# Seven products in place of eight for the right half of a branch projection, in a one-core hybrid block

## The chip, the cores and the metric

The kernel runs on one core of one Trainium2 chip. The metric is the device time of one execution, in microseconds. The engines named below are PE (TensorE, with PEld for its weight loads), DVE (VectorE), ACT (ScalarE), POOL (GpSimd) and SP (SyncE, which here only issues DMAs).

## What is computed

A block of a streaming encoder: 16 meta tokens and 256 frames of 2048 channels, float32, pass through an attention branch and a short-convolution branch; both are projected by a 2048x2048 matrix, gated, added and projected once more. The part that the change touches is `y_att`, the 256x2048 by 2048x2048 product.

```python
def hybrid_layer(x, norm_g, w_in, b_f, conv_w, w_att_o, w_conv_o, w_out):
    h = rmsnorm(x, norm_g)
    proj = jnp.einsum('bld,dn->bln', h, w_in)
    (q, k, v, f_logit, z_att, u, gate_b, gate_c, z_conv,
     m_att, m_conv) = jnp.split(proj, _split_points(), axis=-1)
    ...
    o_att = forgetting_attention(heads(q), heads(k), heads(v), log_f)
    y_att = jnp.einsum('blc,cd->bld', o_att * jax.nn.silu(z_att), w_att_o)
    o_conv = gate_b * short_conv(gate_c * u, conv_w)
    y_conv = jnp.einsum('blc,cd->bld', o_conv * jax.nn.silu(z_conv), w_conv_o)
    merged = jax.nn.sigmoid(m_att) * y_att + jax.nn.sigmoid(m_conv) * y_conv
    return x + jnp.einsum('bld,de->ble', merged, w_out)
```

## The kernel before

**Precision.** A float32 product is made of three matmuls: high part by high part, high by low, low by high. ACT rounds each weight to its high part (`round_unit`, the rows of L610), DVE subtracts to get the low part (`split_unit`, L934), PE does the three matmuls (`product`, L1478 to L1480; `wide_product` does the same work in two matmuls, L1492 to L1495).

**Units.** All weights come in units of 128x1024 floats (512 KB). A unit lands in one of 4 slots of `w_raw` by a DMA on SP's queue, is rounded into `w_hi` and split into `w_lo`, and is used by PE, which then counts up `w_used`. `w_hi` and `w_lo` each have room for 8 units (`RING`). During the convolution stage three of the eight hold other data (`quads`), so the ring has 5 slots (`CONV_RING`) up to unit `U_F`, and 8 from there on. A unit c may be rounded once the unit that held its slot before, c-8 (or c-5), is used: this is the wait on `w_used` in `round_unit`, with the value of `slot_reused(c)`. SP loads unit c once unit c-4 is split.

**Stages.** In the order of time: the convolution stage with six groups of gate columns done by Strassen's seven products (to 618 us), the forget gate and the convolution branch's projection (`U_WC`, to 706 us), the attention stage (`U_ATT`), the attention branch's projection (`U_WA`), the output projection (`U_OUT`), and the last norm.

**Attention stage.** Eight pairs of heads; each pair takes 12 units, 4 for K, 4 for Q and 4 for V. ACT and DVE go through the positions j = 1 to 12 of a pair: at each, first the rounding (ACT) or the split (DVE) of the unit that lies `LEAD` = 5 ahead, then whatever stands at that position. The work on the pair before (`finish_pair`) is hung into the next pair: PE transposes V after its first unit (j = 0), transposes the probabilities after its second, and after its fourth (j = 3) transposes z and multiplies V by the probabilities. ACT and DVE copy and split the transposed probabilities at position 3, and DVE then frees their banks (`free[C]`), for which PE's transposes of z wait. At position 5 DVE makes `gate`, `joined` and `prod2`, at position 6 the low part of `o`. At position 8 DVE adds up q (`join`) once PE has done 8 units, ACT rounds it, DVE makes `q_lo`, and PE waits for that (`q_split`) after its tenth unit, before the scores.

**Branch projection.** `natural` goes through four column blocks of 512 (`nb`), 8 units each; a unit is 2 tiles of k by 2 of tokens by 3 matmuls, 12 matmuls of 512 columns. The last pair of heads is finished inside the first block; its unit j waits for the low part of `o` of pair j (`o_split`). When a block is done DVE multiplies it by the gate and adds `partial` (`merged`), PE transposes the sum (`turn_m`, 8 transposes, after the second unit of the next block), and ACT and DVE round and split it for the output projection.

**Order.** The order on every engine is written out by hand; semaphores alone hold the engines together.

## Time and profile before

| what | value |
|---|---|
| median of 3 runs | 1209.2 us (1209.2 to 1209.27) |
| profiled execution, its own time | 1209.7 us |
| its span (first to last instruction) | 1207.9 us |
| PE busy | 1196.3 us, 99% |
| PE weight loads | 1070.2 us, 89% |
| DVE busy | 925.3 us, 77% |
| ACT busy | 651.9 us, 54% |
| DMA traffic | 280.40 MB, mean 232 GB/s |
| attention stage | 706 to 1018.8 us |
| branch projection of the attention | 1019 to 1112.4 us |

The profile is of one execution. A PE row's start is exact, its end is modelled, so the spacing of starts tells what a matmul costs. The waits that PE shows come to 4.5 us in all, none of them between 618 and 1112 us.

### The profile page before, as it was taken

What the parts mean: (1) busy time and instruction counts of PE and PEld (TensorE: products, weight loads), DVE (VectorE), ACT (ScalarE), POOL (GpSimd) and SP (SyncE); (2) the same over time, 40 slices, a digit from 0 to 9 for tenths busy, and PEclk for the clock granted to TensorE, in tenths of its full rate; (3) what the DMA queues carried; (4) which work ended last, traced back from release to release, by engine and by line L of the source; (5) the groups of instructions that cost most, each with busy time, mean ns of one, the idle gap of its engine ahead of it and who ended that gap; (6) DMA issues with size and microseconds to landing.
All of it is one profiled execution on the core that took longest, in us unless ns stands there. A gap on an engine that the chain in (4) does not pass through costs nothing.

```text
span 1207.9 us, 18425 instructions
## 1 busy us (share of the span) xinstructions
PE 1196.3 (99%) x7252; PEld 1070.2 (89%) x7252; DVE 925.3 (77%) x1095; ACT 651.9 (54%) x868; POOL 35.2 (3%) x50
## 2 busy tenths in 40 slices
PE   9999999999999999999999999999999999999997
PEld 8998898898888988889888899999999999888886
DVE  6989988988989989999966556767676667655544
ACT  7666555556656566656555445445544554543533
POOL 1000000000000000000000010111011101000000
PEclk9999999999999999999999999999999999999999
DMA  6788898898888898898678866556655655665663
GB/s 214 240 294 278 270 297 262 274 300 260 272 289 291 270 292 287 270 309 272 192 238 266 269 184 180 155 180 176 188 155 177 181 170 169 223 207 177 212 227 118
DMA packets 181249, 280.40 MB, mean 232 GB/s; under 512 B 9296, under 2 KB 128160, under 8 KB 180768
## 3 DMA queue, kind: packets, MB, share of 16 engines
q1 hardware_dynamic: 171760, 263.49, 68.3%
q10 hardware_dynamic: 9408, 15.78, 4.2%
q8 instruction: 57, 0.93, 0.3%
q14 instruction: 24, 0.20, 0.1%
HBM read 270.83 MB, written 8.41 MB: 231 GB/s over the span
## 4 chain that ended last, share of the span: by engine, by line
PE 87%; DVE 10%; issue 1%; ACT 1%; DMA 0%; ACTq 0%; POOLq 0%; POOL 0%; DVEq 0%
PE ps L1478 22%; PE ps L1480 22%; PE ps L1479 22%; PE ps L1494 7%; PE ps L1493 6%; PE ps L1495 3%; PE ps L1492 3%; DVE w_lo L1052 2%; DVE w_lo L1089 2%; DVE w_lo L1086 2%; DVE quads L1068 1%; DVE quads L1070 1%; DVE quads L1066 1%; DMA chan_rows<-in_norm_gain 0%; PE ps L1503 0%
## 5 line engine op out<-in xcount | busy, mean ns | idle before, releaser
L934 DVE TENSOR_TENSOR w_lo<-w_raw,w_hi 128x1024 fp32r<-128x1024 f32 x196 | 238.8, 1236 | 99.6 <-ACT w_hi L610 98.9
L1478 PE MATMUL ps<-h,w_hi 128*128 128x258 f32 (+1 forms) x1024 | 293.6, 287 | 1.4 <-DVE w_lo L1052 1.2
L1479 PE MATMUL ps<-h,w_hi 128*128 128x258 f32 (+1 forms) x1024 | 291.2, 284 | 0.0
L1480 PE MATMUL ps<-h,w_lo 128*128 128x258 f32 (+1 forms) x1024 | 290.9, 284 | 0.0
L610 ACT CAST w_hi<-w_raw 128x1024 fp32r<-128x1024 f32 x198 | 204.3, 1051 | 120.1 <-PE ps L1480 74.8
L1478 PEld LDWEIGHTS ps<-h,w_hi 128*128 128x128 f32 x1024 | 192.7, 188 | 5.4 <-issue 1.8
L1479 PEld LDWEIGHTS ps<-h,w_hi 128*128 128x128 f32 x1024 | 192.9, 188 | 2.1
L1480 PEld LDWEIGHTS ps<-h,w_lo 128*128 128x128 f32 x1024 | 192.8, 188 | 0.0
L1052 DVE TENSOR_TENSOR w_lo<-w_raw,w_hi 128x1024 fp32r<-128x1024 f32 x122 | 148.7, 1220 | 15.9 <-ACT w_hi L666 15.7
L1494 PE MATMUL ps<-h,w_hi 128*128 128x512 f32 x408 | 159.9, 397 | 1.0 <-DVE w_lo L1052 0.9
L666 ACT CAST w_hi<-w_raw 128x1024 fp32r<-128x1024 f32 x122 | 127.0, 1049 | 29.2 <-PE ps L1480 25.1
L1493 PE MATMUL ps<-h,w_hi 128*128 128x512 f32 x360 | 142.5, 396 | 0.0
L1495 PE MATMUL ps<-h,w_lo 128*128 128x256 f32 x408 | 113.4, 278 | 0.0
L682 ACT CAST w_hi<-quads 128x1024 fp32r<-128x1024 f32 x48 | 50.6, 1053 | 110.5 <-DVE quads L1068 105.0
L1492 PE MATMUL ps<-h,w_lo 128*128 128x256 f32 x360 | 100.3, 279 | 0.0
L1478 PE MATMUL ps<-w_hi,o 128*128 128x512 f32 x256 | 100.2, 391 | 0.0
L1480 PE MATMUL ps<-w_hi,o 128*128 128x512 f32 x256 | 99.7, 389 | 0.0
L1479 PE MATMUL ps<-w_lo,o 128*128 128x512 f32 x256 | 99.6, 389 | 0.0
L1495 PEld LDWEIGHTS ps<-h,w_lo 128*128 128x128 f32 x408 | 76.7, 188 | 14.7
L1494 PEld LDWEIGHTS ps<-h,w_hi 128*128 128x128 f32 x408 | 77.3, 190 | 6.1 <-DVE w_lo L1052 2.2
L1492 PEld LDWEIGHTS ps<-h,w_lo 128*128 128x128 f32 x360 | 67.6, 188 | 16.4
L1478 PE MATMUL ps<-w_hi,s_hi 128*128 128x512 f32 x192 | 75.1, 391 | 0.0
(211 smaller groups left out, 2055.2 us busy)
## 6 DMA issues: line engine op xcount, KB each, us to landing
w_raw<-in_w_in SPq DMA_DIRECT2D x226, 512.0 KB, 4.9
quads<-in_w_in SPq DMA_DIRECT2D x144, 512.0 KB, 4.5
w_raw<-in_w_conv_o SPq DMA_DIRECT2D x32, 512.0 KB, 5.7
w_raw<-in_w_att_o SPq DMA_DIRECT2D x32, 512.0 KB, 4.6
w_raw<-in_w_out SPq DMA_DIRECT2D x32, 512.0 KB, 4.5
quads<-in_w_in SPq DMA_DIRECT2D x48, 256.0 KB, 5.0
gates_dram<-stage ACTq DMA_DIRECT2D x24, 256.0 KB, 4.9
gate_nat<-gates_dram ACTq DMA_DIRECT2D x8, 512.0 KB, 4.1
```

The lines of the kernel that those rows point to most:

```text
L610: nc.scalar.copy(w_hi[:, hi_slot(c), :], w_raw[:, c % RAW, :]).then_inc(w_rounded, 1)
L666: nc.scalar.copy(w_hi[:, hi_slot(c), :], w_raw[:, n % RAW, :]).then_inc(w_rounded, 1)
L682: nc.scalar.copy(w_hi[:, hi_slot(c), :], quads[:, q, 0, :]).then_inc(w_rounded, 1)
L934: nc.vector.tensor_tensor(w_lo[:, lo_slot(c), :], w_raw[:, c % RAW, :], w_hi[:, hi_slot(c), :].bitcast(F32), ALU.subtract).then_inc(w_spli ...
L1052: nc.vector.tensor_tensor(w_lo[:, lo_slot(c), :], w_raw[:, n % RAW, :], w_hi[:, hi_slot(c), :].bitcast(F32), ALU.subtract).then_inc(w_spli ...
L1478: nc.tensor.matmul(dst, a_hi, b_hi, start=start, stop=False, skip_group_check=resumed)
L1479: nc.tensor.matmul(dst, a_hi, b_lo, start=False, stop=False, skip_group_check=resumed)
L1480: return nc.tensor.matmul(dst, a_lo, b_hi, start=False, stop=stop, skip_group_check=resumed)
L1492: nc.tensor.matmul(dst[:, HI, :], a_lo, b[:, HI, :], start=False, stop=False)
L1493: return nc.tensor.matmul(dst, a_hi, b, start=False, stop=stop)
L1494: nc.tensor.matmul(dst, a_hi, b, start=start, stop=False)
L1495: return nc.tensor.matmul(dst[:, HI, :], a_lo, b[:, HI, :], start=False, stop=stop)
```

## The change

The left half of the columns of `w_att_o` (two blocks of 512) is projected as before. For the right half, seven products take the place of eight: with two column blocks, two token tiles and pairs of k tiles as the 2x2 blocks, `WA_ORDER` has 16 units of the old kind (`n`, 12 matmuls each) and 28 new ones (`a`, `t1`, `b`, `t2`, `b22`, 6 matmuls each); the stage has 44 units where it had 32.

The sums that this needs are made in the attention stage. For each pair, SP loads 1 MB of `w_att_o` (`load_t`) behind the pair's first load, DVE makes four sums of 128x512 (`sum_t`: three at position 7, one at position 9), and SP stores the 1 MB to HBM (`store_t`). Of the activations DVE makes four sums of 128x128 at position 6 (`os_sum`), ACT rounds them at position 7, DVE makes their low part at position 8, and SP stores 512 KB for each pair (`store_os`); POOL's queue fetches seven of them (3.7 MB) when the attention stage ends. PE's first `t1` unit waits for that.

The sums lie where three slots of the `w_hi` ring were. So `hi_slot` and `slot_reused` now use 5 slots up to `U_WIDE`, half way through the output projection, in place of `U_F`; and in the attention stage and behind it the lead is 4 units (`LEAD_5`).

In the branch stage the gate of the first left block is still made at position 8 (`GATE_STEPS`), the first `merged` follows there, and PE transposes it after its unit 10 (`M_TURN`); the last two blocks are put together from the products (`combine`, `merge_products`) at the start of the output projection, whose order is now 8, 4 and 4 tiles of k for each half.

```diff
-OUT_STEP = 8
-OUT_K = OUT_STEP // 2
+
+U_WIDE = U_OUT + 16
...
 def hi_slot(c):
-    return (c - U_F) % CONV_RING if c < U_F else (c + 5) % RING
+    return (c - U_WIDE) % CONV_RING if c < U_WIDE else (c - U_WIDE + CONV_RING) % RING
...
 def slot_reused(c):
 
-    return RING + c - (CONV_RING if c < U_F else RING) + 1
+    return RING + c - (CONV_RING if c < U_WIDE else RING) + 1
...
+        M_TURN = (LEFT_END + 3, RIGHT_END + 4, N_WA + 2, N_WA + 4)
+        M_ROUND = (LEFT_END + 4, RIGHT_END + 5, N_WA + 3, N_WA + 5)
+        GATED = (LEFT_END + 1, RIGHT_END + 1, N_WA, N_WA + 3)
         CONV_STEPS = 4
         ATT_STEPS = 6
-        FIRST_GATE_LOAD, FIRST_GATE_STEP = 5, 8
+        LEAD_5 = LEAD - 1
...
+            def load_t(i):
+
+                if i > 1:
+                    sp.wait_ge(t_stored[i % 2], i // 2 * 16)
+                sp.dma_start(t_quads[:, i % 2, :, :, :], w_att_k[:, 2 * i:2 * i + 2, UNIT:D].rearrange(
+                    "p k (n c) -> p k n c", n=2)).then_inc(t_landed[i % 2], 16)
...
+            pool.wait_ge(w_used, RING + U_WA)
+            pool.wait_ge(os_stored, (PAIRS - 1) * 16)
+            nc.gpsimd.dma_start(os[:, 0:PAIRS - 1, :, :, :].rearrange("p i s n t -> p i (s n t)"),
+                                os_dram.rearrange("i p x -> p i x")).then_inc(os_landed, 16)
...
+                if j == 7:
+                    act.wait_ge(os_made, (i + 1) * 4)
...
+                    nc.scalar.copy(dst, os_sum[:]).then_inc(os_rounded, 1)
 
             for i in range(PAIRS):
                 for j in range(1, N_ATT + 1):
-                    round_unit(None, 0, U_ATT + i * N_ATT + j + LEAD)
+                    if i > 0 or j > 1:
+                        round_unit(None, 0, U_ATT + i * N_ATT + j + LEAD_5)
...
+                    nc.vector.tensor_tensor(os_sum[:, S1, :], a22, a21, ALU.subtract).then_inc(os_made, 1)
+                    nc.vector.tensor_tensor(os_sum[:, S3, :], a11, a21, ALU.subtract).then_inc(os_made, 1)
...
             for i in range(PAIRS):
                 steps = i * ATT_STEPS
                 for j in range(1, N_ATT + 1):
-                    split_unit(None, 0, U_ATT + i * N_ATT + j + LEAD)
+                    if i > 0 or j > 1:
+                        split_unit(None, 0, U_ATT + i * N_ATT + j + LEAD_5)
                     if i > 0:
                         finish_pair(i - 1, j)
+                    if j == 7:
+                        for part in range(3):
+                            sum_t(i, part)
+                    if j == 9:
+                        sum_t(i, 3)
...
+                elif kind == "a":
+                    product(p1, *o_piece(2 * first, 0), *w(left), **ends(first))
+                    last = product(p2, *o_piece(2 * first + 1, 0), *w(right), **ends(first))
+                elif kind == "t1":
+                    product(p5_, *os_piece(S1, 2 * first), *w(left), **ends(2 * first))
+                    last = product(p5_, *os_piece(S1, 2 * first + 1), *w(right), **ends(2 * first + 1))
+                elif kind == "b":
+                    product(p2, *o_piece(2 * first + 1, 1), *w(left), **ends(first))
+                    last = product(p7, *os_piece(S3, first), *w(right), **ends(first))
+                elif kind == "t2":
+                    product(p1, *os_piece(S2, 2 * first), *w(left), **more(2 * first))
+                    last = product(p1, *os_piece(S2, 2 * first + 1), *w(right), **more(2 * first + 1))
+                else:
+                    product(p5_, *os_piece(S4, 2 * first), *w(left), **more(2 * first))
+                    last = product(p5_, *os_piece(S4, 2 * first + 1), *w(right), **more(2 * first + 1))
```

How DVE's row of work changes in a pair of the attention stage, from the end of position 4 to `q_lo` (L939 and L1061 are `join` in the two files; `w_lo` rows are splits of units). Before:

```order
L1297 TENSOR_TENSOR k_lo<-ps,k_hi 128x544 [waits kq_rounded]
L934 TENSOR_TENSOR w_lo<-w_raw,w_hi 128x1024 [waits w_rounded]
L1273 SCALAR_TENSOR_TENSOR gate<-gate,ps 128x512 [waits z_tanh]
L939 TENSOR_REDUCE joined<-ps 128x512 [waits pv_done]
L1279 SCALAR_TENSOR_TENSOR prod_54<-joined,gate 128x512 [waits free_c,free_e]
L934 TENSOR_TENSOR w_lo<-w_raw,w_hi 128x1024 [waits w_rounded]
L1283 TENSOR_TENSOR o<-prod_54,o 128x512 [waits o_rounded]
L934 TENSOR_TENSOR w_lo<-w_raw,w_hi 128x1024 [waits w_rounded] x2
L939 TENSOR_REDUCE joined<-ps 128x512 [waits w_used]
L1305 TENSOR_TENSOR q_lo<-joined,q_hi 128x512 [waits kq_rounded,free_a]
```

Between the low part of `o` and `q_lo` on DVE there stood two splits and the `join`. Now, in DVE's row from the low part of `o` on:

```order
L1402 TENSOR_TENSOR o<-prod_54,o 128x512 [waits o_rounded]
L1407 TENSOR_TENSOR os_sum<-prod_54 128x128
L1408 TENSOR_TENSOR os_sum<-prod_54 128x128
L1410 SCALAR_TENSOR_TENSOR os_sum<-os_sum,prod_54 128x128 [waits os_made]
L1413 SCALAR_TENSOR_TENSOR os_sum<-prod_54,os_sum 128x128 [waits os_made]
L1056 TENSOR_TENSOR w_lo<-w_raw,w_hi 128x1024 [waits w_rounded]
L1427 TENSOR_TENSOR t_quads<-t_quads 128x512 [waits t_landed1]
L1429 TENSOR_TENSOR t_quads<-t_quads 128x512
L1432 TENSOR_TENSOR t_quads<-t_quads 128x512 [waits t_summed]
L1056 TENSOR_TENSOR w_lo<-w_raw,w_hi 128x1024 [waits w_rounded]
L1418 TENSOR_TENSOR os_pair<-os_sum,os_pair 128x512 [waits os_rounded]
L1061 TENSOR_REDUCE joined<-ps 128x512 [waits w_used]
```

Four sums of 128x128, three of 128x512 and one low part of 128x512 have come in ahead of the `join`; `q_lo` follows it as before.

On PE, the first transposes of `merged` in the branch stage stood between two units of the second block, after its second unit, behind 24 matmuls since the first block's end. Before:

```order
L1480 MATMUL ps<-w_hi,o 128x512
L1478 MATMUL ps<-w_hi,o 128x512
L1479 MATMUL ps<-w_lo,o 128x512
L1480 MATMUL ps<-w_hi,o 128x512
L1472 MATMUL ps<-ident,merged 128x128 [waits merged_made]
L1472 MATMUL ps<-ident,merged 128x128 x7
L1478 MATMUL ps<-w_hi,o 128x512 [waits w_split]
```

Now on PE they stand behind the first `t1` unit:

```order
L1672 MATMUL ps<-w_hi,os 128x512 [waits w_split,os_landed]
L1673 MATMUL ps<-w_lo,os 128x512
L1674 MATMUL ps<-w_hi,os 128x512
L1672 MATMUL ps<-w_hi,os 128x512
L1673 MATMUL ps<-w_lo,os 128x512
L1674 MATMUL ps<-w_hi,os 128x512
L1666 MATMUL ps<-ident,merged 128x128 [waits merged_made]
L1666 MATMUL ps<-ident,merged 128x128 x7
L1672 MATMUL ps<-w_hi,o 128x512 [waits w_split,free_b]
```

Between the first block's end and these transposes there are now three units of 6 matmuls: 18.

## Rows read from the trace of the kernel before

**Rows 1.** The page, part 1: busy us, share of the span, instructions.

```profile
PE 1196.3 (99%) x7252; PEld 1070.2 (89%) x7252; DVE 925.3 (77%) x1095; ACT 651.9 (54%) x868; POOL 35.2 (3%) x50
```

**Rows 2.** The waits of PE: total us, times, longest; first and last of four.

```profile
PE ps L1503 <- POOL ident L565: 1.9, 1, 1.9
...
PE ps L1589 <- DMA chan_rows<-in_norm_gain: 0.5, 1, 0.5
```

**Rows 3.** Windows: length, busy us of each engine, clock, DMA share, GB/s.

```profile
9.00:12.00 3.00, 3.00 (x16) 2.63 (x15) 1.68 (x6) 2.70 (x6) 0.56 (x2) 1.00 1.08 382
...
330.00:360.00 30.00, 30.00 (x178) 26.60 (x178) 25.20 (x31) 18.23 (x25) 0.00 (x0) 1.00 0.90 289
...
862.00:901.00 39.00, 39.00 (x293) 37.44 (x293) 26.49 (x34) 18.77 (x35) 3.86 (x4) 1.00 0.58 175
```

**Rows 4.** Timeline of PE in a branch unit: start us, us, engine, line.

```profile
1107.62 0.39 PE L1478 MATMUL ps<-w_hi,o 128*128 128x512 f32 x1
...
1111.70 0.39 PE L1478 MATMUL ps<-w_hi,o 128*128 128x512 f32 x1
```

**Rows 5.** Timeline of PE in one pair: third unit's start, z's transposes, scores.

```profile
867.84 0.37 PE L1478 MATMUL ps<-h,w_hi 128*128 128x272 f32 x1
...
873.86 0.60 PE L1678 MATMUL ps<-ident,z_nat 128*128 128x128 f32 x4
...
892.77 0.23 PE L1478 MATMUL ps<-k_hi,q_hi 128*128 128x144 f32 x1
```

**Rows 6.** Timeline of ACT in the same pair.

```profile
868.12 0.80 ACT L828 CAST probs_t<-ps 128x768 fp32r<-128x768 f32 x1 [1.08 <-PE ps L1670]
...
874.06 0.61 ACT L854 CAST k_hi<-ps 128x544 fp32r<-128x544 f32 x1 [3.26 <-PE ps L1480]
874.57 1.05 ACT L610 CAST w_hi<-w_raw 128x1024 fp32r<-128x1024 f32 x1
875.51 0.60 ACT L836 ACTIVATE gate<-ps 128x512 f32<-128x512 f32 x1
...
881.53 1.05 ACT L610 CAST w_hi<-w_raw 128x1024 fp32r<-128x1024 f32 x1 [0.58 <-PE ps L1493]
```

**Rows 7.** Timeline of DVE in the same pair.

```profile
870.72 0.40 DVE L1266 SCALAR_TENSOR_TENSOR p_tail<-ps,tail_row,p_tail 32x32 fp32r<-32x32 f32 x2
...
875.65 1.23 DVE L934 TENSOR_TENSOR w_lo<-w_raw,w_hi 128x1024 fp32r<-128x1024 f32 x1 [0.22 <-ACT w_hi L610]
...
878.64 0.69 DVE L1279 SCALAR_TENSOR_TENSOR prod<-joined,gate 128x512 f32<-128x512 f32 x1
879.25 1.53 DVE L934 TENSOR_TENSOR w_lo<-w_raw,w_hi 128x1024 fp32r<-128x1024 f32 x1
...
881.88 2.35 DVE L934 TENSOR_TENSOR w_lo<-w_raw,w_hi 128x1024 fp32r<-128x1024 f32 x2
887.05 1.22 DVE L939 TENSOR_REDUCE joined<-ps 128x512 f32<-128x1024 f32 x1 [2.81 <-PE ps L1493]
889.03 0.69 DVE L1305 TENSOR_TENSOR q_lo<-joined,q_hi 128x512 fp32r<-128x512 f32 x1 [0.76 <-ACT q_hi L857]
```

**Rows 8.** Groups by line: count, busy us, mean ns; small operations of DVE.

```profile
L1258 DVE TENSOR_TENSOR v_tail<-ps,v_tail 32x256 fp32r<-32x256 f32 x8 | 3.3, 416 | 0.1
...
L1319 DVE TENSOR_SCALAR nmax<-smax 128x4 f32<-128x4 f32 x8 | 1.4, 170 | 0.3
```

**Rows 9.** Timeline of DVE in the branch stage.

```profile
1036.57 0.69 DVE L1283 TENSOR_TENSOR o<-prod,o 128x512 fp32r<-128x512 f32 x1
...
1044.57 1.22 DVE L1243 TENSOR_TENSOR merged<-ps,gate_nat 128x1024 f32<-128x1024 f32 x1 [3.08 <-PE ps L1480]
1045.83 1.23 DVE L1356 TENSOR_TENSOR merged<-merged,partial 128x1024 f32<-128x1024 f32 x1
```

**Rows 10.** Timeline of ACT in the branch stage: position 8.

```profile
1039.18 1.05 ACT L610 CAST w_hi<-w_raw 128x1024 fp32r<-128x1024 f32 x1 [1.67 <-PE ps L1480]
...
1041.55 1.06 ACT L801 ACTIVATE gate_nat<-gate_nat 128x1024 f32<-128x1024 f32 x1
```

More of the change, by code:

```diff
@@ L102 @@
 HI, LO = 0, 1
-OUT_BANK = (4, 0)
+OUT_BANK = (0, 4)
 A, B, C, E = 0, 2, 4, 6
@@ L1358, in _ @@
-            split_m(NB - 1)
-            rest = UNITS - (U_OUT + 1 + LEAD)
-            with dve.Fori(0, rest // RING) as i:
-                for j in range(RING):
-                    split_unit(i, RING, U_OUT + 1 + LEAD + j)
-            for n in range(UNITS - rest % RING, UNITS):
-                split_unit(None, 0, n)
+                nc.vector.tensor_tensor(merged[:], ps[:, bank:bank + 2, :], gate_wa[:, nb, :, :], ALU.mult
+                                        ).then_inc(free[bank], 1)
```

373 lines of the change are left out of this document (285 added, 88 removed).

## The prediction, made before the changed kernel had run

> **What bounds the kernel now.** I read the page's shares first: PE is busy 99% of the span [rows 1]. Matmul busy time alone does not show that PE is at its limit, so the waits come next: PE waits 1.9 us for its first operand and 0.5 us for another at the start, 4.5 us in all, and in the attention and branch stages not once [rows 2]. A window of one pair in the attention stage shows PE busy all 39.00 us, DVE 26.49, ACT 18.77, DMA at 175 GB/s [rows 3]. So every matmul taken away shortens the kernel by its spacing, and every wait put on PE lengthens it by its length. DVE has a third of its time free, but that is an average: what counts is how early the results for which PE waits are made. The timelines of one pair [rows 5 to 7] tell that, so the prediction is made from them.
>
> **What is removed.** 18 matmuls of a branch unit start within 1107.62 to 1111.70 us, 0.2267 us each [rows 4]. Before, the right half took 16 units of 12, 192 matmuls; now 28 units of 6, 168. That is 24 x 0.2267 = **5.4 us less** on PE. No transposes come or go.
>
> **What the shorter ring does in the attention stage.** Before, at position j ACT rounded unit j+5 into a slot last held by the unit eight earlier. Now it rounds unit j+4 into a slot last held by unit j-1, five earlier (units counted from 0), and so cannot start position j before PE has ended unit j-1. Before, it could start when unit j-3 had ended. That this wait is real can be seen before the change: at 881.53 ACT starts a rounding released by PE, which is position 8 waiting for unit 5 [rows 6]. Everything that stands at a position now comes up to two units (5.5 us) later against PE. Two of PE's own waits depend on it.
>
> **First wait: the transposes of z (after PE's fourth unit).** They start at 873.86; two units before them started at 867.84, so a unit is 3.01 us and unit 2 ends at 870.85 [rows 5]. They need `free[C]`, freed by DVE at position 3, at 870.72 + 0.40 = 871.12, so 2.7 us of slack [rows 7]. After the change position 3 starts when unit 2 has ended. ACT follows PE by 0.20 (874.06 after 873.86 [rows 5, 6]); the rounding keeps it 0.94 (874.57 to 875.51); from its copy of the probabilities (868.12) to DVE's end at 871.12 are 3.00 [rows 6, 7]. The way back to PE I take as 0.08, an estimate between the 0.03 that DVE follows ACT by (874.57 + 1.05, then 875.65) and the 0.20 of PE to ACT. Sum 0.20 + 0.94 + 3.00 + 0.08 = 4.22, against one unit of 3.01: PE waits **1.21 us**, in 7 pairs, 8.5 us. The eighth time is in the branch stage, where a unit is 12 x 0.2267 = 2.72: 1.50 us.
>
> **Second wait: q for the scores (after the tenth unit).** ACT sees unit 5 end at 881.53 and DVE sees unit 7 end at 887.05, so a Q unit is 2.76 and unit 4's end was seen at 878.77; the scores start at 892.77, 14.00 after that [rows 5 to 7]. DVE's `q_lo` is ready at 889.03 + 0.69 = 889.72, slack 3.05. Now position 5 starts at unit 4's end, and DVE has work in one row from there: rounding and start of the split 1.08 (874.57 to 875.65); that split, gate, `joined`, `prod2`, the next split and the low part of `o` 6.23 (875.65 to 881.88); the four sums of 128x128; a split 1.22, of which 0.08 overlaps the next (as 0.69 takes 0.61 from 878.64 to 879.25), so 1.14; three sums of 128x512 at 0.61, 0.72 (the next one waits for its end) and 0.61, 1.94; a split 1.14; the low part of the sums 0.61; from the `join` to the end of `q_lo` 2.67 (887.05 to 889.72); 0.08 [rows 6, 7]. No row shows a 128x128 sum. It lies between a 128x4 operation, 170 ns, and a 32x256 one, 416 ns [rows 8]; by size nearer the middle, and I take 0.26 each with the waits between them, 1.05 (bounds 0.68 and 1.66). Sum 15.94, less 14.00: PE waits **1.94 us**, in the 7 pairs that have a pair before them, 13.6 us; by the bounds 11.0 to 17.9. The first pair has no pair to finish: from unit 6's end 1.08 + 1.14 + 1.94 + 1.14 + 2.67 + 0.08 = 8.05 against 14.00 - 2 x 2.76 = 8.48, no wait. Could these two waits hide each other? No: each is counted from a unit's end that is later than the wait before it.
>
> **Branch stage, two more.** The eighth unit waits for the low part of the last pair's `o`. From unit 4's end: 0.20 + 1.08 + 3.60 (875.65 to 879.25) + 1.14 + 0.69 [rows 9] + 0.08 = 6.79, against two units, 5.44: **1.35 us**. Then the first transposes of `merged`: position 8 starts at the first block's end; ACT's rounding, table load and gate take from 1039.18 to 1041.55 + 1.06 = 1042.61, 3.43 [rows 10]; DVE's two steps from 1044.57 to 1047.06, 2.49 [rows 9]; with 0.20, 0.03 and 0.08 the sum is 6.23. PE has only 18 matmuls to do, 4.08 us, where it had 24: it waits **2.15 us**. Together with the 1.50 above the branch stage gets 5.0 us of waits.
>
> **Edits at nothing.** Behind the last product DVE has its split, four combining steps and two of `merged`, ended 7.6 us after PE's last branch matmul (0.20 + 0.94 + a copy of 0.6, then 2.65 to 3.3 for the four sums at 0.69, then 2.5); PE transposes after three output units, 8.16, so 0.5 is spare. If that cover is gone the cost is what exceeds it. DMA in the attention stage: 2.5 MB more per pair is 64 GB/s on 175; the stage before ran at 289 with PE busy 30.00 of 30.00 [rows 3]. SP's stores stand behind loads that are issued four units after the sums are made, so they hold up no load; `load_t` is issued after position 4's split and has some 12 us to land (8 in the first pair). ACT's new copy, 0.6 us at position 7, ends before DVE's three sums do.
>
> **Sum.** -5.4 + 8.5 + 13.6 + 5.0 = **+21.7 us**. On the profiled execution: span 1207.9 to 1229.6, its time 1209.7 to 1231.4. The median of the runs is 0.5 lower, so 1209.2 + 21.7 = **1230.9 us**.
>
> **Rivals.**
> Only the first wait (1217.3 us). If DVE's row of work in positions 5 to 8 is 2 us shorter than summed, the second wait goes and its 13.6 with it. For it: 1.94 in 15.94 is a small difference of a long sum, and the split at 879.25 lasted 1.53 where others last 1.22 to 1.23 [rows 7], so some of the 6.23 is contention that may fall elsewhere. Against: four 128x128 sums at the least possible price still leave 1.6.
> All hidden (1203.8 us, faster than before). The mechanism is DVE's and ACT's spare third: the results for the z transposes and the scores are made within the slack they have now, 2.7 and 3.05 us, and the branch stage likewise. It decides at 3.01 us for the first chain, which I sum to 4.22, and at 14.00 for the second. For it: PE waits nowhere here before, and the 5.4 us are certain. Against: the ring's wait on `w_used` can be seen in [rows 6].
> Weights late as well (1234.6 us). A 6-matmul unit takes 1.36 us and 0.524 MB, 385 GB/s. At the 289 GB/s of the convolution stage [rows 3] a unit takes 1.81. The last 19 units (16 short, 3 long) and 8 transposes take PE 30.8 us; the loads 34.4, 3.6 more, less what the ring has ahead. POOL's 3.7 MB come in the first ten units. Against: three microseconds at 382 GB/s [rows 3], and eight units are ahead when the short ones begin. The Trainium skill, DMA: Bandwidth & Descriptors, Specifications, gives about 358 GB/s as the HBM limit of one core. By it 0.524 MB takes an estimated 1.46 us, 0.10 more than PE needs, and 28 units give at most 2.8 us; the row at 382 shows that this case has gone above that for 3 us.
>
> **Chances.** The forecast 0.57; only the first wait 0.18; weights late as well 0.14; all hidden 0.09; 0.02 for a result that happens to fall on no change. Range: with the bounds of the small sums the forecast is 1228.3 to 1235.2, with late weights up to 1239; the lower end takes in the 1217.3. I give 1215 to 1240, which leaves out the 1203.8 and 0.05 of mishaps. A difference under 0.2% is about what a measurement cannot tell from none: faster 0.09, within 0.02, slower 0.89.
>
> **What would show it.** PE's waits in the changed profile: the transposes of z waiting for DVE's `p_tail` 8 times at 1.2 to 1.5 us, the scores waiting for `q_lo` 7 times near 1.9, a branch matmul waiting once for `o`, the transposes of `merged` once near 2.1. A pair should take 3.15 us longer than before. ACT should wait for PE ahead of nearly every rounding. If a pair is only 1.2 longer, the second chain is mis-sized; if PE waits for `w_lo` in the short units, weights are late. The granted clock stays 1.00 in the windows if waits of this length leave it alone; a lower one would make the forecast too low.

## The result, and the profile after

The changed kernel takes 1252.6 us (median of four runs, 1250.4 to 1255.3) against 1209.2 before: ratio 1.036, 95% interval 1.034 to 1.038. The forecast was 1230.9 us with a range of 1215 to 1240. The direction was right. The size was wrong by 21.7 us, as much again as was forecast, and the time lies outside the range.

The profiled execution has a span of 1251.1 us, 43.2 more than before. Its page begins with the busy time of the engines, which answers to [rows 1]:

```profile
span 1251.1 us, 18110 instructions
## 1 busy us (share of the span) xinstructions
PE 1206.2 (96%) x7228; PEld 1074.8 (86%) x7228; DVE 973.7 (78%) x1184; ACT 672.1 (54%) x891; POOL 36.0 (3%) x51
```

PE issues 24 matmuls fewer and is nevertheless busy for 10 us longer. Waiting alone can't do that: waits show up in the idle time, not in the busy time. So two things happened, waits and slower matmuls. First the waits of PE (waiting line, what released it, us in total, times, longest), which answer to [rows 2]:

```profile
PE ps L1672 <- DVE q_lo L1461: 11.2, 7, 1.6
PE ps L1872 <- DVE p_tail L1385: 8.6, 7, 1.2
PE ps L1666 <- DVE merged L1501: 6.6, 3, 4.1
PE ps L1872 <- DMA z_nat<-gates_dram: 3.3, 1, 3.3
PE ps L1672 <- DVE left_c L1555: 1.5, 1, 1.5
PE ps L1672 <- DVE o L1402: 1.2, 1, 1.2
PE ps L1672 <- DVE w_lo L1056: 0.9, 1, 0.9
```

The first two rows and the sixth are waits of the forecast. The fourth, the fifth, the last and most of the third are not: a late transfer, a late product, a late weight, and a wait of 4.1 us where 0.5 us was said to be spare.

Then the windows (PE, PEld, DVE, ACT and POOL busy with counts, granted clock, DMA share, GB/s). The first is the pair of [rows 3], the other two follow one of the waits for `q_lo`:

```profile
862.00:901.00 39.00, 36.17 (x267) 34.20 (x266) 27.19 (x42) 19.20 (x34) 3.88 (x4) 1.00 0.70 227
952.00:954.00 2.00, 2.00 (x14) 2.00 (x13) 2.00 (x4) 0.00 (x0) 0.00 (x0) 0.66 0.38 57
954.00:956.00 2.00, 2.00 (x10) 2.00 (x10) 1.96 (x3) 0.00 (x0) 0.00 (x0) 0.50 0.97 312
```

In the first window, 39 of a pair's 43 us, PE is idle for 2.8 us, at full clock. Around 954 it is never idle, but the granted clock is 0.50, that is 1.2 GHz instead of 2.4, and 10 matmuls start in 2 us. The timeline of PE shows the change of pace (start, duration, line, operation, shapes; in brackets the idle time ahead and its releaser):

```profile
948.97 0.28 PE L1674 MATMUL ps<-h,w_lo 128*128 128x272 f32 x1
950.85 0.33 PE L1672 MATMUL ps<-k_hi,q_hi 128*128 128x144 f32 x1 [1.60 <-DVE q_lo L1461]
...
952.37 0.28 PE L1672 MATMUL ps<-h,w_hi 128*128 128x272 f32 x1
952.49 0.31 PE L1673 MATMUL ps<-h,w_hi 128*128 128x272 f32 x1
...
953.05 0.43 PE L1673 MATMUL ps<-h,w_hi 128*128 128x272 f32 x1
953.28 0.43 PE L1674 MATMUL ps<-h,w_lo 128*128 128x272 f32 x1
```

PE stood still from 949.25 to 950.85 and went on at full pace (0.12 us from one matmul to the next). From about 952.6 it needed 0.23 us for each. This happened six times while PE had work, each time for some 3.4 us, and each time at a wait: behind four of the seven waits for `q_lo` (at 778, 952, 997 and 1041), behind the wait for `z_nat` (1065), and from 1160.8 on, in the last half microsecond of the last wait for `merged`. Working through 3.4 us at half pace costs 1.7 us, so six cost some 10 us. In the profile before, the clock falls only after PE's last matmul.

The span divides like this; pairs are counted from one transpose of `v_t` to the next. The last pair's `v_t` is transposed from 1022.3 before and from 1052.0 now, the first pair's from 744.4 and 745.0:

| stretch | more than before | made of |
|---|---|---|
| up to the first pair's `v_t` | 0.6 | start-up and unchanged code; the profiles of all the kernels here differ by up to 2.6 |
| seven pairs | 29.1 | 7 x 3.2 of waits, 4 x 1.7 of half clock |
| last pair, branch, output | 13.5 | -5.4 of matmuls, 13.5 of waits, 2 x 1.7 of half clock, 2.0 more (seven waits, after which PE takes 0.2 to 0.3 to get going) |

The forecast had 22.1 for the second row and -0.4 for the third.

### The profile page after: what moved, and what is told of

It is laid out like the page before. It is cut to its first block, busy times and chain, and to the rows that moved or that the text cites. A ratio compares the mean times of both kernels' runs of the same rounds, so it can differ in the third digit from the quotient of the medians.

```text
span 1251.1 us, 18110 instructions
## 1 busy us (share of the span) xinstructions
PE 1206.2 (96%) x7228; PEld 1074.8 (86%) x7228; DVE 973.7 (78%) x1184; ACT 672.1 (54%) x891; POOL 36.0 (3%) x51
## 4 chain that ended last, share of the span: by engine, by line
PE 68%; DVE 20%; DMA 5%; ACT 4%; issue 2%; ACTq 0%; POOLq 0%; POOL 0%; DVEq 0%; SPq 0%
PE ps L1672 18%; PE ps L1674 17%; PE ps L1673 17%; PE ps L1688 5%; DVE w_lo L1056 4%; PE ps L1687 4%; PE ps L1689 3%; DMA w_raw<-in_w_att_o 2%; DVE w_lo L1174 2%; ACT w_hi L722 2%; PE ps L1686 2%; DVE w_lo L1211 2%; DVE w_lo L1208 2%; DVE joined L1061 1%; DVE quads L1190 1%
## 5 line engine op out<-in xcount | busy, mean ns | idle before, releaser
L1056 DVE TENSOR_TENSOR w_lo<-w_raw,w_hi 128x1024 fp32r<-128x1024 f32 x208 | 255.9, 1236 | 190.5 <-ACT w_hi L722 189.3
L722 ACT CAST w_hi<-w_raw 128x1024 fp32r<-128x1024 f32 x210 | 218.5, 1049 | 250.9 <-PE ps L1674 161.6
L1674 PE MATMUL ps<-h,w_lo 128*128 128x258 f32 (+1 forms) x1024 | 293.5, 287 | 0.0
L1672 PEld LDWEIGHTS ps<-h,w_hi 128*128 128x128 f32 x1024 | 195.5, 191 | 5.4 <-issue 1.8
L1673 PEld LDWEIGHTS ps<-h,w_hi 128*128 128x128 f32 x1024 | 195.6, 191 | 2.1
L1174 DVE TENSOR_TENSOR w_lo<-w_raw,w_hi 128x1024 fp32r<-128x1024 f32 x122 | 148.8, 1220 | 15.9 <-ACT w_hi L778 15.7
L778 ACT CAST w_hi<-w_raw 128x1024 fp32r<-128x1024 f32 x122 | 126.9, 1049 | 28.2 <-PE ps L1674 25.1
L1672 PE MATMUL ps<-w_hi,o 128*128 128x512 f32 x216 | 85.0, 393 | 2.7 <-DVE left_c L1555 1.5
L1673 PE MATMUL ps<-w_lo,o 128*128 128x512 f32 x216 | 84.3, 390 | 0.0
L1674 PE MATMUL ps<-w_hi,o 128*128 128x512 f32 x216 | 84.2, 390 | 0.0
L1688 PEld LDWEIGHTS ps<-h,w_hi 128*128 128x128 f32 x408 | 77.3, 190 | 6.1 <-DVE w_lo L1174 2.2
```

What stands on the lines that cost most here:

```text
L722: nc.scalar.copy(w_hi[:, hi_slot(c), :], w_raw[:, c % RAW, :]).then_inc(w_rounded, 1)
L778: nc.scalar.copy(w_hi[:, hi_slot(c), :], w_raw[:, n % RAW, :]).then_inc(w_rounded, 1)
L1056: nc.vector.tensor_tensor(w_lo[:, lo_slot(c), :], w_raw[:, c % RAW, :], w_hi[:, hi_slot(c), :].bitcast(F32), ALU.subtract).then_inc(w_spli ...
L1174: nc.vector.tensor_tensor(w_lo[:, lo_slot(c), :], w_raw[:, n % RAW, :], w_hi[:, hi_slot(c), :].bitcast(F32), ALU.subtract).then_inc(w_spli ...
L1672: nc.tensor.matmul(dst, a_hi, b_hi, start=start, stop=False, skip_group_check=resumed)
L1673: nc.tensor.matmul(dst, a_hi, b_lo, start=False, stop=False, skip_group_check=resumed)
```

## The experiments

### The ring alone

The kernel before, with the changed slot count and the lead of four, and nothing of the new products:

```diff
+U_WIDE = U_OUT + 16
-    return (c - U_F) % CONV_RING if c < U_F else (c + 5) % RING
+    return (c - U_WIDE) % CONV_RING if c < U_WIDE else (c - U_WIDE + CONV_RING) % RING
...
-                    round_unit(None, 0, U_ATT + i * N_ATT + j + LEAD)
+                    if i > 0 or j > 1:
+                        round_unit(None, 0, U_ATT + i * N_ATT + j + LEAD - 1)
```

> The kernel before with the shorter ring alone: five slots up to the sixteenth output unit, rounding one unit less ahead; no weight sums, no stores, the right half of the branch projection as before. Theory of the ring (waits come from positions that start up to two units later): the transposes of z wait 1.2 us in seven pairs and 1.5 us in the branch stage, the fifth wait in the branch stage 1.35 us, the first transposes of merged 0.8 us; the scores do not wait, since without the sums DVE's row from the end of the fifth unit is 12.3 us against 14.0. Sum 12.2 us, 1221.4 us. Theory of the clock: it fell only behind waits in the changed kernel; if a wait of 1.2 us is enough, some of these eight show half clock and up to 1.7 us more each comes on top; if only those of 1.6 us and more do it, the clock stays whole and the time is 1221. Rival (the waits come from DVE's sums, not from the ring): no waits and 1209 us.

Measured: 1222.9 us against 1208.8 in the same session, ratio 1.011 (1.010 to 1.013). PE's waits, and the window of a pair:

```profile
PE ps L1671 <- DVE p_tail L1262: 10.0, 8, 1.5
PE ps L1471 <- DVE o L1279: 1.2, 1, 1.2
PE ps L1465 <- DVE merged L1353: 0.7, 1, 0.7
```

```profile
862.00:901.00 39.00, 37.77 (x281) 36.03 (x280) 25.80 (x34) 18.94 (x34) 3.86 (x4) 1.00 0.52 162
```

All three waits of the ring stand there with the forecast sizes (10.0 for 8.5 + 1.5, 1.2 for 1.35, 0.7 for 0.8), and the scores don't wait. The granted clock stays whole throughout the attention and branch stages: none of the nine waits of 1.2 to 1.5 us was followed by half clock in this execution.

### A wait alone, in the kernel before

Is the half clock caused by PE standing still, or by something else in the changed kernel? Here only DVE gets more to do, so that PE waits 2 us in seven pairs:

```diff
+                        if i > 0:
+                            for n in range(7):
+                                nc.vector.tensor_tensor(q_lo[:], k_hi[:, :, 0:SEQ].bitcast(F32),
+                                                        k_hi[:, :, 0:SEQ].bitcast(F32), ALU.subtract
+                                                        ).then_inc(extra, 1)
+                                dve.wait_ge(extra, 7 * (i - 1) + n + 1)
                         join(bank, joined)
```

> The kernel before with one thing added: in seven pairs DVE does seven more operations of 128x512, each waiting for the one before (0.72 us apiece, 5.0 in all), between the end of q's projection and the join of q. q_lo has 3.05 us of slack, so PE waits 2.0 us seven times, 14 us in all, with the ring, the units and the transfers as before. Theory of the clock (half clock follows PE's standing still for about this long, sometimes): some of these seven waits are followed by half clock for some 3.4 us, at 1.7 us each: 1223 us and 0 to 12 us more, 1226 to 1233, with a spread from run to run. Rival (the dips of the changed kernel come from something else in it, its transfers or DVE's load): the clock stays whole and the time is 1223 in every run.

Measured: 1230.2 us (1229.3 to 1230.9) against 1210.1, ratio 1.017 (1.015 to 1.018). The wait, and windows behind two of the seven:

```profile
PE ps L1485 <- DVE q_lo L1312: 13.8, 7, 2.3
```

```profile
778.00:780.00 2.00, 2.00 (x13) 2.00 (x12) 1.97 (x3) 0.24 (x1) 0.00 (x0) 0.59 0.51 106
...
904.00:906.00 2.00, 2.00 (x14) 2.00 (x13) 2.00 (x2) 1.69 (x2) 0.00 (x0) 0.66 0.00 0
906.00:908.00 2.00, 2.00 (x11) 2.00 (x11) 1.97 (x4) 0.00 (x0) 0.00 (x0) 0.50 0.80 224
```

Three of the seven waits were followed by half clock, in a kernel that has neither the ring nor the new products nor their transfers. The window from 904 moved no bytes at all. The excess of 20.1 us is 7 x 2.15 of waiting and 3 x 1.7 of half clock.

### The same waits, filled

Sixteen transposes of the identity ahead of each of these waits; they touch nothing but the bank that the scores overwrite:

```diff
-                        pe.wait_ge(q_split, i + 1)
                         pe.wait_ge(free[C], FREE_C["att"] + 3 * i)
+                        if i > 0:
+                            for _ in range(16):
+                                nc.tensor.transpose(ps[:, C, 0:P], ident[:], ident[:])
+                        pe.wait_ge(q_split, i + 1)
```

> The kernel with the wait alone (d1_wait_alone), in which PE stood still seven times for 2 us and the clock halved three times, with sixteen transposes of the identity on PE ahead of each of these waits; at 0.11 us each they fill 1.8 of the 2.0 us, and the scores start at the same time as without them. Theory (half clock follows PE's standing still): no dip in the attention stage in the profiled run, and the time falls from 1230.2 by the three dips at 1.7 us, to 1225 us. Rival (the clock fell for DVE's added work or by chance): dips as before and 1230 us.

Measured: 1224.5 us (1224.4 to 1225.2) against 1208.9, as expected to half a microsecond.

```profile
PE ps L1485 <- DVE q_lo L1312: 1.6, 7, 0.5
```

The idle time at the scores went from 13.8 to 1.6 us, and the attention stage has no window under 1.00. The delay for the scores is still there, because DVE's added work is; only the half clock has gone. The seven pairs take 293.5 us against 298.1, 4.6 less, where three stretches were worth 5.1. The medians differ by 5.7, of which 1.2 is between the two sessions: the kernel before took 1210.1 in one and 1208.9 in the other. The four runs lie 0.7 us apart instead of 1.5.

### Fillers in the changed kernel

The same edit in the changed kernel, with twelve transposes.

> The changed kernel with twelve transposes of the identity on PE ahead of its wait for q_lo in seven pairs, written into the scores' bank before the scores. They fill some 1.4 to 1.8 us in which PE would stand still and nothing else is moved. Theory of the clock (half clock for 3.4 us follows PE's standing still): the dips at the scores, four of six in the profiled run, go, and the time falls by 4 x 1.7 = 6.8 us at most, less up to 0.2 us for each pair in which the fillers outlast the wait: 1246 to 1249 us, and closer together from run to run. Rival (the clock falls for a reason other than the wait): dips as often as before, 1252 or more.

Measured: 1247.7 us (1246.7 to 1250.5), 4.9 less than the changed kernel.

```profile
PE ps L1672 <- DVE q_lo L1461: 1.9, 7, 0.3
```

In the profiled execution no half clock is left at the scores; three stretches remain later, at the waits for `z_nat` (3.8 us here), for `left_c` (2.2) and for `merged` (3.8), and one stands at the start. The first of them is twice as long (6.8 us, 3.4 lost). So the seven pairs are 6.3 us shorter (300.7 for 307.0) and the rest is 2.2 longer (201.3 for 199.1), which is why the median gives only 4.9. The clock theory holds in both kernels.

### The weight sums behind q

```diff
-                    if j == 7:
+                    if j == 9:
                         for part in range(3):
                             sum_t(i, part)
-                    if j == 9:
+                    if j == 11:
                         sum_t(i, 3)
...
-                if j == 6 and 0 <= i - 1 < PAIRS:
+                if j == 8 and 0 <= i - 1 < PAIRS:
                     store_t(i - 1)
```

> The changed kernel with the four weight sums later in a pair: three at position 9 and one at 11, behind q_lo, and their store two loads later. Theory (the score wait is DVE's row of work between the end of the fifth unit and q_lo, of which the three sums are 1.94 us): the wait for q_lo falls from 1.6 us of idle time (1.9 by spacing) to at most 0.2, 13 us in seven pairs, and the four dips of the clock that stood behind it go as well, up to 6.8 us: 1233 to 1240 us. The wait for p_tail stays at 1.2 us, seven times. Rival (the clock falls of its own, without the waits): as many dips as in the changed kernel, 1239 to 1240. Second rival (something other than DVE's row holds q_lo): 1252 as before.

Measured: 1249.5 us, four runs at 1243.2, 1244.4, 1254.6 and 1254.9; the profile is of the one at 1254.6. None of the three expectations names what happened:

```profile
PE ps L1872 <- DMA z_nat<-gates_dram: 19.0, 8, 5.5
...
PE ps L1672 <- DVE q_lo L1461: 1.8, 7, 0.3
```

The wait for `q_lo` went as the theory said, from 11.2 to 1.8 us, so DVE's row of work is what held it. In its place stands a wait for z, eight times. The median time from issue to landing of z's 0.26 MB, the middle figure of this row, is 8.2 us here, 4.7 in the changed kernel and 3.7 before (lowest, median, highest):

```profile
DMA to landing us min/median/max: 7.9/8.2/11.6
```

In one pair the 1 MB store of the sums was issued at 831.65 and z's fetch at 835.07; the windows between them and z's landing near 843 run at a DMA share of 0.91 to 1.09:

```profile
834.00:836.00 2.00, 2.00 (x19) 1.98 (x18) 0.44 (x2) 1.32 (x2) 0.00 (x0) 1.00 1.07 403
```

With the store two loads later it collides with z's fetch, which has no slack. The expectation had named the later store and given it no price. The waits for z, up to 5.5 us long, were followed by half clock too, four times in the attention stage and once, for twice as long, for the last pair; the last wait for `merged` had one of twice the length as well.

### The pair's steps first

```diff
+                    if i > 0:
+                        finish_pair(i - 1, j)
                     if i > 0 or j > 1:
                         round_unit(None, 0, U_ATT + i * N_ATT + j + LEAD_5)
...
-                    if i > 0:
-                        finish_pair(i - 1, j)
```

and the same on DVE with `split_unit`, in the attention stage only.

> The changed kernel with the order on ACT and DVE turned at each position of the attention stage: first the steps of the pair before, then the rounding and the split of the weights, so that only the weights wait for the slot. The branch stage is as it was. Theory (both waits exist only because the pair's steps stand behind a rounding that waits for a slot): the transposes of z no longer wait in the six pairs inside the loop, and the scores wait 0.5 us at most, although the three sums stay in front of q_lo: 8.6 + 11 to 13 us less, and up to 6.8 us of clock dips: 1224 to 1233 us. Rival (DVE has too much work in a row at these positions whatever stands first): the score wait stays above 1.5 us and the time above 1240.

Measured: 1223.6 us (1221.1 to 1227.3; the profile is of the lowest), ratio 1.013 to before: 29 us less than the changed kernel from an exchange of two calls, on ACT and on DVE. The same window of a pair, and PE's waits, in which no row of the attention stage is left:

```profile
862.00:901.00 39.00, 39.00 (x290) 37.23 (x290) 29.90 (x46) 19.76 (x34) 2.88 (x4) 1.00 0.72 237
```

```profile
PE ps L1666 <- DVE merged L1501: 5.9, 2, 3.9
PE ps L1872 <- DMA z_nat<-gates_dram: 3.0, 1, 3.0
...
PE ps L1672 <- DVE left_c L1555: 1.8, 1, 1.8
```

DVE does all its sums (29.90 us busy) and PE never waits for it. So the second wait isn't a want of DVE time: it is the row of work standing behind a rounding that waits for a slot. The seven pairs now take 279.7 us, 1.8 more than before. What is left above the kernel before lies from the last pair on: 196.8 us against 185.6.

### z ahead of the fetch of the activation sums

The changed kernel, with one line on POOL ahead of its fetch:

```diff
             pool.wait_ge(os_stored, (PAIRS - 1) * 16)
+            pool.wait_ge(z_landed, PAIRS * 16)
```

> The changed kernel with one wait more: GpSimd's fetch of 3.7 MB of activation sums starts when the last pair's z has landed. Theory (the z fetch of 0.26 MB took 9.5 us to land because the 3.7 MB ran beside it): z lands in some 5 us, PE's wait for it, 3.3 us, shrinks to the wait for p_tail of 1.3 us, and the dip of the clock behind it may go with it: 2 to 4 us less, 1249 to 1251 us. Rival (the other loads alone fill the transfers): the wait stays at 3 us and the time within 1 us of 1252.6. If the sums then come too late for their first product, a wait for os appears in its place.

The rows behind it, from the changed kernel: the issues of both fetches (all eight of z, the last at 1055.2; the one of POOL at 1049.3), and the transfers in the ten microseconds after z's issue:

```profile
L928 ACTq DMA_DIRECT2D z_nat<-gates_dram x8: 378/447/1009, 749.3 to 1055.2; - x8
```

```profile
L702 POOL DMA_DIRECT2D os<-os_dram x1: 1122/1122/1122, 1049.3 to 1049.3; - x1
```

```profile
1056.00:1066.00 10.00, 6.71 (x31) 5.33 (x31) 6.05 (x8) 4.94 (x11) 0.00 (x0) 0.96 1.10 396
```

Measured: 1249.2 us (1247.0 to 1250.8), 3.5 less than the changed kernel. The longest of z's eight landings fell from 9.5 to 5.0 us, and the wait became one for `p_tail`:

```profile
PE ps L1873 <- DVE p_tail L1386: 10.1, 8, 1.5
```

So the eighth z was late because 3.7 MB were under way beside it; without them the eighth wait is 1.5 us, as forecast. The Trainium skill says in DMA: Bandwidth & Descriptors, Issuing engines are not separate DMA queues, that DMAs of all issuing engines run on the same 16 engines and interleave; by that rule a fetch issued by POOL delays one of ACT, and the trace agrees (9.5 us to land beside it, 5.0 without).

### Copies and combining ahead of the rounding

The kernel with the pair's steps first, and in the branch and output stages ACT's copies of the products ahead of `round_unit`, DVE's `combine` and `merge_products(2)` ahead of `split_unit`, and the transposes of `merged` one or two units later (shown here; `M_ROUND` and `GATED` follow them):

```diff
-        M_TURN = (LEFT_END + 3, RIGHT_END + 4, N_WA + 2, N_WA + 4)
+        M_TURN = (LEFT_END + 4, RIGHT_END + 5, N_WA + 3, N_WA + 6)
```

> The kernel with the pair's steps first in the attention stage (the third experiment), and in the branch and output stages two things changed: ACT's copies of finished products and DVE's combining stand ahead of the rounding and the split of their position, and the transposes of merged come one to two units later on PE. Theory (the waits for merged and for left_c are chains that stand behind a rounding which waits for a late weight): of the 1.8 + 5.9 us of these waits at least 5.5 go, and a dip of 1.7 with them: 1223.5 - 5.5 to 9.4 = 1214 to 1218 us. Rival (the chains are bound by the late products themselves, or the later rounding makes the output weights late): the waits move to the output units and the time stays above 1220.

What suggested it was this place in the changed kernel, where the last branch matmul had ended at 1147.9 and the copy of the product by ACT, the first step of the combining, stands behind a rounding that waits for its weights:

```profile
1153.73 1.05 ACT L722 CAST w_hi<-w_raw 128x1024 fp32r<-128x1024 f32 x1 [0.83 <-DMA w_raw<-in_w_out]
1154.69 0.57 ACT L1018 COPY left_c<-ps 128x512 f32<-128x512 f32 x1
...
1154.82 1.23 DVE L1056 TENSOR_TENSOR w_lo<-w_raw,w_hi 128x1024 fp32r<-128x1024 f32 x1 [0.66 <-ACT w_hi L722]
1155.96 0.68 DVE L1521 TENSOR_TENSOR right_c<-left_c,ps 128x512 f32<-128x512 f32 x1
...
1161.31 1.97 PE L1666 MATMUL ps<-ident,merged 128*128 128x128 f32 x8 [4.15 <-DVE merged L1501]
```

Measured: 1223.7 us, the same as the kernel that it builds on (1223.6); in the profiles the part from the last pair on is 197.1 us against 196.8. The waits only changed their names:

```profile
PE ps L1675 <- DVE m_lo L1546: 3.0, 2, 2.7
PE ps L1675 <- DVE w_lo L1056: 2.5, 1, 2.5
...
PE ps L1669 <- DVE merged L1501: 0.5, 1, 0.5
```

`merged` fell from 5.9 to 0.5 and `left_c` from 1.8 to 0.5, and `m_lo` and `w_lo` took 5.5 in their place. The rival was right: this order had decided only which result is late.

### All of it together

The steps first in the branch stage too, and POOL's fetch behind z.

> All of it together: the pair's steps first in the attention stage and for the last pair in the branch stage too, copies and combining first, the transposes of merged later, and GpSimd's fetch behind z. Theory (every microsecond above the 5.4 saved is one of the waits named): from 1223.5 go 3.0 (z), 1.2 (o), 1.8 (left_c), 5.9 (merged) and 1.7 of clock, 13.6 at most, and what remains is PE's late weights in the short units: 1209.9 us at the least, 1210 to 1215. Rival (a floor above that, since the short units need weights at more than the transfers bring): 1216 and more, with waits for w_lo in the branch stage's second half.

Measured: 1220.9 us (1220.2 to 1222.1), ratio 1.009. The time is the rival's, above 1216. How high the floor lies isn't shown by it: an order further down takes 1216.3 with the same bytes.

```profile
PE ps L1676 <- DVE w_lo L1057: 3.6, 1, 3.6
PE ps L1676 <- DVE m_lo L1547: 2.9, 1, 2.9
```

Behind the first of them stands one load of the stored sums. It was issued at 1064.98, and ACT's rounding of it started at 1073.22, after 4.2 us of standing still (ACT's waits for such loads from 1056 to 1082: total, times, longest):

```profile
ACT w_hi L723 <- DMA w_raw<-t_dram: 6.4, 3, 4.2
```

At these two waits there was half clock, for 6.8 us and for 3.4, which is 5.1 us lost.

### Half the bytes in the short units

On this kernel, the loads of the 28 short units bring half. The other half of a slot keeps what it held, so this kernel leaves out part of the weights and doesn't compute the product; it is there for its time only.

```diff
+            def load_half(c, src):
+
+                sp.wait_ge(w_split, c + 1)
+                dst = w_raw[:, c % RAW, :].rearrange("p (k n) -> p k n", k=2)[:, 0:1, :]
+                sp.dma_start(dst, src).then_inc(w_landed[c % RAW], 16)
...
-                    load(None, 0, U_WA + n, w_att_k[:, 2 * first:2 * first + 2, UNIT:UNIT + HALF], k=2)
+                    load_half(U_WA + n, w_att_k[:, 2 * first:2 * first + 1, UNIT:UNIT + HALF])
```

> The seventh kernel (e7_all) with half the bytes in each load of the 28 short units of the branch projection: 0.26 MB instead of 0.52, the other half of the slot keeps what it held, so that part of the weights is left out of what is computed, and no instruction on PE, ACT or DVE changes. Theory (what remains over the 5.4 saved in the branch and output stages is weights that the transfers bring late, and the chains that stand behind their rounding): the waits for w_lo (3.6 us) and m_lo (2.9 us) and the dips behind them (about 3.5 us) go: 1220.9 - 6.5 to 10 = 1211 to 1214 us. Rival (the waits come from the ring and the order alone, with weights that would be in time): the time stays within 1.5 us of 1221.

Measured: 1210.1 us (1209.3 to 1212.2), ratio to before 1.001 (1.000 to 1.002), that is 10.8 us less than with whole loads, and no half clock in the branch stage. The waits for `w_lo` fell from 3.6 to 0.3 and for `m_lo` from 2.9 to 1.5. Forty microseconds of the branch stage with whole loads, and then the same with half loads:

```profile
1064.00:1104.00 40.00, 36.42 (x148) 29.08 (x148) 23.55 (x20) 22.28 (x23) 0.00 (x0) 0.91 0.79 263
```

```profile
1064.00:1104.00 40.00, 39.66 (x176) 32.11 (x175) 29.34 (x26) 25.86 (x27) 0.00 (x0) 1.00 0.63 193
```

In this order the late transfers cost the 10.8 us, the half clock behind them included, although over 40 us they are busy 0.79 and not 1.00. An average share below 1 doesn't mean that weights are in time. Each load waits for its place in the four raw slots, so at the pace of a short unit (1.36 us) four loads in flight may take an estimated 5.4 us to land. The median for the stored sums is 5.9 with whole loads and 3.5 with half (5.1 in the changed kernel, where the longest took 11.7), and ACT's waits for them show the same, whole loads first:

```profile
ACT w_hi L723 <- DMA w_raw<-t_dram: 15.9, 13, 4.2
```

```profile
ACT w_hi L728 <- DMA w_raw<-t_dram: 2.9, 3, 1.9
```

That the time to land decides, and not the bytes in all, is an argument from these rows: the half loads change both.

### Two more orders

With the rounding and split of `merged`'s transposes ahead of the weights as well:

> The seventh kernel (e7_all) with the rounding and the split of merged's transposes ahead of the rounding and the split of the weights as well, and the second transposes of merged back where the changed kernel has them, one unit earlier. Theory (the wait of 2.9 us for m_lo at the first output unit is a chain behind a late rounding): it goes, and the 3.6 us for w_lo stay: 1218 to 1219 us. Rival (conserved: what is late is the weights, and any chain moved ahead of them makes them later): a wait for w_lo grows by as much and the time stays at 1221.

Measured: 1216.3 us (1215.2 to 1218.3), 4.5 less. The wait for `m_lo` is gone, and three waits for `w_lo`, 3.8 us in all, stand beside 2.5 for `merged`. The time is better than both expectations. This profile has no half clock in the branch stage, where the kernel it builds on lost 5.1 us to it; that is about as much as the gain. Then with POOL's fetch cut into three:

```diff
+            for n, (lo, hi) in enumerate(((0, 2), (2, 4), (4, PAIRS - 1))):
+                pool.wait_ge(w_used, RING + U_WA + (0, 5, 10)[n])
```

> The tenth kernel (e10_m_first) with the fetch of 3.7 MB of activation sums cut into three, for two, two and three pairs, started at the branch stage's units 0, 5 and 10. Theory (the single fetch takes the transfers from the weights of the first ten units): the wait of 3.6 us for w_lo near the tenth unit goes or falls under 1 us, with its dip: 3 to 6 us less than the tenth kernel, 1213 to 1216 us. Rival (a load of the stored sums is slow by itself: one took 8.2 us to land where the median is 5.4): the wait stays and the time is that of the tenth kernel.

Measured: 1216.7 us, no difference, as the rival had it. The waits for `w_lo` grew from 3.8 to 5.7 us in all:

```profile
PE ps L1678 <- DVE w_lo L1059: 5.7, 4, 3.0
```

The bytes are the same and only their time moved; late weights are still there. The best corrected form takes 1216.3 us: 36 us less than the change as made, and 6.4 more than the kernel before in the same session (1209.9). No version here beats the kernel before.

## Why the prediction was wrong in size

**What is removed: 5.4 us.** Not disputed by any run, but never seen on its own. The kernel with half loads, in which nearly nothing waits, needs 184.2 us from the last pair on, against 185.6 before: 1.4 less, with 2.3 of waits left in it. About 1.7 of the 5.4 I can't account for.

**First wait: right.** Forecast 1.21 us seven times; measured 8.6 us of idle time in seven. The ring alone has the same wait and, with the one in the branch stage, 10.0 in eight.

**Second wait: right.** Forecast 1.94; measured 11.2 us of idle time in seven, 1.6 each, with PE's start-up about 1.9. A pair without half clock is 3.2 us longer, forecast 3.15. The small sums, which no row had shown, took 0.28 to 0.29 us, the first of the four this (lowest, median, highest in ns):

```profile
L1407 DVE TENSOR_TENSOR os_sum<-prod x7: 277/279/280, 769.1 to 1031.4; 128x128 f32<-128x128 f32 x7
```

They were taken at 0.26 each, 1.05 for the four with the waits between them; in the first pair that has them they go from 769.11 to the next split at 770.03, 0.92. The sum had the late start behind the slot and the longer row in it, and the runs show that it takes both: with the ring alone, or with the three sums behind `q_lo`, the wait is gone or down to 0.3 us. What the forecast didn't ask is whether the row has to stand behind the rounding.

**The failed step, first part: the clock.** The prediction said: "The granted clock stays 1.00 in the windows if waits of this length leave it alone; a lower one would make the forecast too low." It put the condition down and gave it no price and no chance. The trace of before couldn't price it: after the start PE's longest wait there is 0.9 us, and no half clock follows it. But a forecast that puts seventeen waits on PE and names the clock as a condition has it as a rival, and it was left out of the sum, of the rivals and of the range. The measured term is six times up to 1.7, some 10 us, nearly half of what was missed. That the standing still causes it is shown by the wait alone (1230.2) and the same wait filled (1224.5). It is probably also why the four runs of the changed kernel lie 4.9 us apart: filling the waits brought the spread from 1.5 to 0.7 us in one pair of kernels and from 4.9 to 3.8 in the other.

**Second part: z in the branch stage.** The forecast had the eighth z wait at 1.50, for `p_tail`; it was 3.3, for the transfer, 1.8 more. I had POOL's 3.7 MB in the sum only as weight traffic, and hadn't asked which small transfer with no slack runs beside them. Shown by the kernel in which z goes first.

**Third part: "so 0.5 is spare".** The wait behind the combining was 4.15 us. The chain's length was nearly right: from ACT's copy at 1154.69 to the transposes at 1161.31 are 6.6 us, and by the forecast's own terms 0.6 + 2.65 to 3.3 + 2.5 = 5.75 to 6.4. What was wrong was its start: 0.20 + 0.94 behind PE's last matmul in the forecast, 6.8 us behind it in fact, since ACT was held up by roundings whose weights were late (the three before the copy had waited 1.93, 0.17 and 0.83 us for `in_w_out`). The priced cover, a rounding of 0.94, was itself waiting for something.

**The rival of late weights.** I gave it 0.14 and 3.6 us, and looked for it in a wait for `w_lo`. That row is 0.9 us, and on that reading the rival had lost. It had in fact come true one step earlier, on ACT. From 1052 to 1165 ACT's roundings waited 27.3 us for loads, the stored sums first (total, times, longest):

```profile
ACT w_hi L722 <- DMA w_raw<-t_dram: 11.9, 12, 2.2
```

On PE that shows under other names: most of the last `merged`, and by the same argument, without a run of its own, `left_c` with 1.5. How much the transfers cost depends on the order: 10.8 us in the kernel on which the half loads were tried, and since a better order alone won 4.5 of them, some 6 in the best one (1216.3 less 1210.1, two kernels that differ in order too). The reason against the rival was "three microseconds at 382 GB/s". The peak was no bound: 396 GB/s held for 10 us here. The rows point to the time to land with four loads in flight, 5.1 us in the median and 11.7 at the longest, for 5.4 allowed. The Trainium skill's figure of 358 GB/s in DMA: Bandwidth & Descriptors, Specifications, is a per-core share, and the row at 396 shows that it didn't bind.

**Right in the branch stage:** `o` 1.2 (forecast 1.35) and the first `merged` 2.0 of its 6.6 (forecast 2.15).

**The parts together.** In the profile 21.5 us were missed, which the rows give to within rounding: some 10 of clock, 1.8 for z, 4.6 for the later `merged`, 2.4 for `left_c` and `w_lo`, some 2 of starts after waits, 0.6 ahead of the first pair and 0.2 in the pairs, less 0.3 where the forecast was high.

## What to carry to other kernels

The shorter buffer ring cost next to nothing by itself (1.8 us in seven pairs, once the order was turned, sums included); it cost what stood on the same engine behind the instruction that waits for a slot. Put what other engines wait for first and the refill last, and check that the cover you count on isn't waiting for a transfer itself. Where a change puts waits on an engine that had none, price the loss of its clock as a term of its own; where a wait can't be removed, harmless work in it gives that part back. When a chain is moved ahead and the time stays, the late thing is elsewhere: halve the bytes and see.

## What the runs showed of the hardware

- PE's waits of 1.6 us for `q_lo` were followed by half clock (1.2 instead of 2.4 GHz) in 4 of 7 cases in the changed kernel, and those of 1.9 to 2.3 us in 3 of 7 in the kernel with the wait alone. Waits of 1.2 to 1.5 us in the attention stage and behind it: none in nine of the changed kernel and none in nine of the ring alone. Behind the waits for `q_lo` the slow stretch began 0.9 to 1.8 us after PE had gone on, so that the row of the wait and the row of the slow matmuls stand apart in the trace.
- At all eight waits of 3.6 to 5.5 us in the profiles (the last `merged` in five kernels, z in two, `w_lo` in one) the clock was halved, in seven of them before the wait had ended. Most stretches lasted some 3.4 us, four of them twice that.
- Between these lengths the length of a single wait doesn't decide it alone. A wait of 3.0 us for z in the kernel with the pair's steps first was not followed by half clock; one of 3.0 in the kernel with copies first and one of 3.3 in the changed kernel were. What else decides is open.
- The same is seen at the kernel's start, in code that no version changes. Where PE waited 1.0 us or more for the norm gains, a stretch of half clock stood between 8 and 13 us, in six of six profiles; where it waited 0.2 to 0.7 us, in none of eight. It explains no difference between kernels here: the six reach the first pair's `v_t` at 743.6 to 744.3 us, the eight at 742.9 to 745.5.
- A 1 MB store issued 3.4 us ahead of a 0.26 MB fetch on another engine's queue held the fetch back: 8.2 us to land in the median for 4.7.
